# A recurrent mixer worked in two halves of four tiles inside one long fp32 transformer kernel

## The reference, cut to what matters

```python
def recurrent_mixer(h, w_in, conv_w, conv_b, w_a, b_a, w_x, b_x, lam, w_out):
    gate, xr = jnp.split(h @ w_in, 2, axis=-1)
    gate = jax.nn.gelu(gate, approximate=True)
    xr = causal_conv(xr, conv_w, conv_b)              # 4 taps along the tokens
    return (rg_lru(xr, w_a, b_a, w_x, b_x, lam) * gate) @ w_out

def rg_lru(x, w_a, b_a, w_x, b_x, lam):               # w_a, w_x: 8 blocks of 128 x 128
    r = sigmoid(blockwise(x, w_a) + b_a)
    i = sigmoid(blockwise(x, w_x) + b_x)
    log_a = 8.0 * r * log_sigmoid(lam)
    a = exp(log_a)
    u = sqrt(-expm1(2.0 * log_a)) * (i * x)
    # scan along the tokens: h_t = a_t * h_(t-1) + u_t
```

## Time and profile before

| what | value |
|---|---|
| median of the three runs | 2420.32 us (2416.55 to 2423.21) |
| the profiled execution's own time | 2414.51 us |
| its span, first to last instruction | 2413.1 us |
| TensorE busy | 2189.7 us, 91% of the span |
| VectorE busy | 1417.7 us, 59% |
| ScalarE busy | 1118.3 us, 46% |
| chain of waits that ended last | TensorE 78%, VectorE 14%, ScalarE 4% |
| mean granted TensorE clock | 0.957 of 2.4 GHz |
| the mixer, from its first transpose to its last matmul | about 2094.7 to 2207.8 us of the span |

### The profile page before, as it was taken

How to read it: one execution, slowest core, us unless ns; L and a number is a source line. 1 busy time by engine, 2 the same in 40 slices (tenths; PEclk the granted TensorE clock), 3 DMA queues, 4 the chain that set the end, 5 groups by cost and what they waited for, 6 DMA issues and landing times.

```text
span 2413.1 us, 25425 instructions
## 1 busy us (share of the span) xinstructions
PE 2189.7 (91%) x10080; PEld 1790.5 (74%) x10080; DVE 1417.7 (59%) x1934; ACT 1118.3 (46%) x1711; POOL 31.9 (1%) x40
## 2 busy tenths in 40 slices
PE   4998879999999878999989999988999999977998
PEld 3785667788778567778878878757788788755886
DVE  2795665555479565555545545765555555546553
ACT  2434435544444443544444445634544444464442
POOL 0000000000000000000000000100000000000000
PEclk8998899999999889999999999999999999998999
DMA  6553124455455312445545554322455455432553
GB/s 199 185 192 122 37 97 147 148 189 189 162 188 193 105 52 90 148 148 189 183 161 191 180 178 175 143 84 86 168 187 182 178 179 190 167 138 109 180 191 122
DMA packets 53277, 371.10 MB, mean 154 GB/s; under 512 B 6439, under 2 KB 6583, under 8 KB 9512
## 3 DMA queue, kind: packets, MB, share of 16 engines
q1 hardware_dynamic: 49248, 358.19, 41.3%
q0 software_dynamic: 1552, 4.20, 0.9%
q10 hardware_dynamic: 2360, 7.09, 0.8%
HBM read 366.31 MB, written 3.15 MB: 153 GB/s over the span
## 4 chain that ended last, share of the span: by engine, by line
PE 78%; DVE 14%; ACT 4%; DMA 2%; issue 1%; POOL 0%; ACTq 0%; DVEq 0%; POOLq 0%
PE ps L434 22%; PE ps L436 22%; PE ps L435 22%; DVE ring_lo L957 4%; DVE acc L1160 3%; PE ps L479 3%; PE ps L528 2%; DMA skew<-acc 2%; PE ps L625 1%; PE ps L684 1%; PE ps L463 1%; PE ps L513 1%; ACT upper_w L1582 1%; ACT z L1638 1%; DVE xn L1092 1%
## 5 line engine op out<-in xcount | busy, mean ns | idle before, releaser
L957 DVE TENSOR_TENSOR ring_lo<-ring,upper_w 128x1024 fp32r<-128x1024 f32 x659 | 804.4, 1229 | 537.7 <-ACT upper_w L1582 533.2
L1582 ACT CAST upper_w<-ring 128x1024 fp32r<-128x1024 f32 x659 | 689.8, 1055 | 582.9 <-PE ps L436 579.3
L434 PE MATMUL ps<-upper_w,nT_hi 128*128 128x512 f32 x1992 | 791.6, 397 | 70.1 <-DVE nT_lo L1540 24.9
L435 PE MATMUL ps<-ring_lo,nT_hi 128*128 128x512 f32 x1992 | 779.5, 391 | 0.0
L436 PE MATMUL ps<-upper_w,nT_lo 128*128 128x512 f32 x1824 | 713.1, 391 | 0.0
L434 PEld LDWEIGHTS ps<-upper_w,nT_hi 128*128 128x128 f32 x1992 | 379.9, 191 | 151.0 <-DVE ring_lo L957 29.9
L435 PEld LDWEIGHTS ps<-ring_lo,nT_hi 128*128 128x128 f32 x1992 | 379.5, 191 | 76.4 <-issue 1.0
L436 PEld LDWEIGHTS ps<-upper_w,nT_lo 128*128 128x128 f32 x1824 | 345.5, 189 | 73.1
L436 PE MATMUL ps<-upper_w,tT_lo 128*128 128x512 f32 (+1 forms) x792 | 309.5, 391 | 0.0
L434 PE MATMUL ps<-upper_w,z_hi 128*128 128x512 f32 x624 | 244.3, 391 | 2.7 <-DVE x L1015 2.7
L435 PE MATMUL ps<-ring_lo,z_hi 128*128 128x512 f32 x624 | 242.8, 389 | 0.0
(11 more groups left out here) (288 smaller groups left out, 1423.6 us busy)
## 6 DMA issues: line engine op xcount, KB each, us to landing
ring<-in_w SPq DMA_DIRECT2D x340, 1024.0 KB, 4.8
big<-in_gains ACTq DMA_DIRECT2D x6, 512.0 KB, 3.7
skew<-acc POOLq DMA_DIRECT2D x1, 2048.0 KB, 46.5
z<-in_mem ACTq DMA_DIRECT2D x2, 1024.0 KB, 6.5
big<-skew POOLq DMA_DIRECT2D x1, 1536.0 KB, 7.8
x<-in_x SPq DMA_DIRECT2D x1, 1024.0 KB, 4.9
out<-x ACTq DMA_DIRECT2D x2, 512.0 KB, 3.1
const<-in_const SPq DMA_DIRECT2D x1, 593.0 KB, 6.3
```

What stands on the lines that cost most here:

```text
L434: PE.matmul(out, hi, w_hi, start=start, stop=False)
L435: PE.matmul(out, hi, w_lo, start=False, stop=False)
L957: V.tensor_tensor(ring_lo[:, q % RING, cols], ring[:, q % RING, cols], upper_w[:, n % AHEAD, :].bitcast(F32), ALU.subtract).then_inc(*lo_c ...
L1582: A.copy(upper_w[:, n % AHEAD, :], ring[:, q % RING, part * HALF:(part + 1) * HALF]).then_inc(*hi_cut.up(h))
```

## The change

The reference and the layout of the inputs stay. What changes lies in the three engines' `recurrent` functions and in the list of the ring's chunks:

- The weights of the sigmoids leave the ring. ScalarE's queue loads them, 1 MB, into `xn`, which is free there, as `gate_w`. The ring has 339 chunks where it had 340.
- Convolution, sigmoids, decay, square root, scan and gelu are done for tiles 0 to 3 (index 0) and tiles 4 to 7 (index 1). Their steps stand as `beside` work between the cuts of `rec.in1`, `rec.in2`, `rec.in3` and the output product. TensorE turns tiles 0 to 3 of the x part behind the first half of `rec.in1`, tiles 4 to 7 behind the first half of `rec.in2`; the eight block matmuls of index 0 stand behind the second half of `rec.in2`, those of index 1 and the first gelu turn behind the first half of `rec.in3`, and the second gelu turn behind the second half of the output product.
- All four taps of the convolution are VectorE's. Exp and tanh take the decay factor as their scale, tile by tile, in place of VectorE's product (L1522).
- The output product has its chunks in another order: input tiles 0 to 3 for columns 0 to 511 (`rec.out0a`) and 512 to 1023 (`rec.out1a`), then tiles 4 to 7 for both (`rec.out0b`, `rec.out1b`).
- The cut-ahead goes on from `rec.in3` into the output product.

The diff, cut to its core (first the chunks, then TensorE, VectorE, ScalarE):

```diff
         w.add(f"rec.in{b}", [at + 2 * b, at + 2 * b + 1])
-    w.end_run("ffn_a.up0", "rec.in3")
-    w.add("rec.gates", [at + 8], split=False)
-    for b in range(2):
-        w.add(f"rec.out{b}", [at + 9 + 2 * b, at + 10 + 2 * b])
+    w.gates = at + 8
+    for part in range(2):
+        for b in range(2):
+            w.add(f"rec.out{b}{'ab'[part]}", [at + 9 + 2 * b + part])
     ffn_stream(w, "ffn_d", at + 13)
-    w.end_run("rec.out0", "ffn_d.down")
+    w.end_run("ffn_a.up0", "ffn_d.down")
...
+    gate_w = xn[:, :, :].rearrange("p t n -> p (t n)")
...
+        def gemm(seg, lhs, banks, ready=(), beside=None, first=0, kts=None):
+
+            if first == 0:
+                free(*banks)
+            kts = kts or 2 * len(W.span[seg])
             for c, h in enumerate(W.span[seg]):
                 w_hi, w_lo = weights(h)
                 for k in range(2):
-                    f, cols = 2 * c + k, slice(k * BLK, (k + 1) * BLK)
+                    f, cols = first + 2 * c + k, slice(k * BLK, (k + 1) * BLK)
...
+            def inputs(i):
+                turn(f"rec.cin{i}", cols_of(z, D + 512 * i), 4, [act_out.at(f"rec.in{i}")], lambda c: act_out.at(f"rec.cin{i}.{c}"))
+
+            def gates(i):
+
+                PE.wait_ge(*gates_loaded.at("gates"))
+                PE.wait_ge(*dve_out.at(f"rec.conv{4 * i + 3}"))
+                free(4, 5, 6, 7)
+                for kind in range(2):
+                    for j in range(4):
+                        c = 4 * i + j
+                        m = PE.matmul(ps[:, 4 + 2 * kind + j // 2, j % 2 * T:(j % 2 + 1) * T], gate_w[:, (8 * kind + c) * P:(8 * kind + c + 1) * P], xT[:, c, :], start=True, stop=True)
+                m.then_inc(*psum_full.up(f"rec.gates{i}"))
+                for j in range(4):
+                    held(act_out.at(f"rec.s{i}.{2 * j + 1}"), 4 + j)
+
+            def gelus(i, banks):
+                turn(f"rec.g{i}", cols_of(z, 512 * i), 4, [act_out.at(f"rec.in{2 + i}")], lambda c: act_out.at(f"rec.g{i}.{c}"), banks=banks)
+            gemm("rec.in0", lhs, (0, 1), n)
+            held(act_out.at("rec.in0"), 0, 1)
+            gemm("rec.in1", lhs, (2, 3), beside=lambda c: inputs(0) if c == 0 else None)
+            held(act_out.at("rec.in1"), 2, 3)
+            work = {0: lambda: inputs(1), 1: lambda: gates(0)}
+            gemm("rec.in2", lhs, (0, 1), beside=lambda c: work.get(c, lambda: None)())
+            held(act_out.at("rec.in2"), 0, 1)
+            gemm("rec.in3", lhs, (2, 3), beside=lambda c: (gates(1), gelus(0, (0, 1))) if c == 0 else None)
+            held(act_out.at("rec.in3"), 2, 3)
             ready = [dve_out.at(f"rec.lo{c // 4}") for c in range(8)]
-            gemm("rec.out0", lhs, (0, 2), ready)
-            gemm("rec.out1", lhs, (1, 3))
+            for part in range(2):
+                for b in range(2):
+                    if b and not part:
+                        gelus(1, (6, 7))
+                    gemm(f"rec.out{b}{'ab'[part]}", lhs, (b, b + 2), ready, first=4 * part, kts=KT)
...
-            if h + AHEAD - 1 <= W.run_end[h]:
-                cut(h + AHEAD - 1)
+            n = W.halves[h][2] + AHEAD - 1
+            if n < len(W.split) and W.split[n] <= W.run_end[h]:
+                cut(W.split[n])
...
+            def conv(c):
+                if c % 4 == 0:
+                    V.wait_ge(*act_out.at(f"rec.cin{c // 4}.2"))
+                if c == 0:
+                    V.wait_ge(*pool_out.at("rec.left"))
+                w = s2("rw")
+                V.tensor_scalar(xT[:, c, :], cin8[:, c, 0:T], w[:, 4 * c:4 * c + 1], s2("rb")[:, c:c + 1], ALU.mult, ALU.add).then_inc(*dve_out.up())
+                for k in range(1, 4):
+                    own()
+                    V.scalar_tensor_tensor(xT[:, c, :], cin8[:, c, k:k + T], w[:, 4 * c + k:4 * c + k + 1], xT[:, c, :], ALU.mult, ALU.add).then_inc(*dve_out.up(f"rec.conv{c}" if k == 3 else None))
+
+            def squared(i):
+                part = parts8[i]
+                V.wait_ge(*act_out.at(f"rec.s{i}.7"))
+                own()
+                V.tensor_tensor(iT[:, part, :], iT[:, part, :], xT[:, part, :], ALU.mult).then_inc(*dve_out.up())
+                V.wait_ge(*act_out.at(f"rec.th{i}"))
                 V.tensor_tensor(rT[:, part, :], aT[:, part, :], aT[:, part, :], ALU.mult).then_inc(*dve_out.up())
                 own()
+                V.scalar_tensor_tensor(th[:, part, :], rT[:, part, :], 1.0, th[:, part, :], ALU.add, ALU.mult).then_inc(*dve_out.up(f"rec.sq{i}"))
+
+            def scanned(i):
+                part = parts8[i]
+                V.wait_ge(*act_out.at(f"rec.root{i}"))
                 V.tensor_tensor(iT[:, part, :], iT[:, part, :], th[:, part, :], ALU.mult).then_inc(*dve_out.up())
                 own()
                 for c in range(part.start, part.stop):
                     V.tensor_tensor_scan(rT[:, c, :], aT[:, c, :], iT[:, c, :], 0.0, ALU.mult, ALU.add).then_inc(*dve_out.up())
                 own()
+                V.wait_ge(*act_out.at(f"rec.g{i}.2"))
+                V.tensor_tensor(nT[:, part, :], rT[:, part, :], gT[:, part, :], ALU.mult).then_inc(*dve_out.up(f"rec.h{i}"))
+
+            def rest(i):
+                part = parts8[i]
+                V.wait_ge(*act_out.at(f"rec.hi{i}"))
+                V.tensor_tensor(nT_lo[:, part, :], nT[:, part, :], nT_hi[:, part, :].bitcast(F32), ALU.subtract).then_inc(*dve_out.up(f"rec.lo{i}"))
+
+            def last_conv():
+                conv(6)
+                conv(7)
+            cuts("rec.in0")
+            work = {1: lambda: conv(0), 2: lambda: conv(1), 3: lambda: conv(2)}
+            cuts("rec.in1", lambda n: work.get(n, lambda: None)())
+            work = {0: lambda: conv(3), 1: lambda: conv(4), 2: lambda: conv(5), 3: last_conv}
+            cuts("rec.in2", lambda n: work[n]())
+            work = {1: lambda: squared(0), 3: lambda: scanned(0)}
+            cuts("rec.in3", lambda n: work.get(n, lambda: None)())
+            rest(0)
+            squared(1)
+            work = {2: lambda: scanned(1), 3: lambda: rest(1)}
+            for n, h in enumerate(h for part in "ab" for b in range(2) for h in W.span[f"rec.out{b}{part}"]):
+                cut_ahead(h)
+                work.get(n, lambda: None)()
...
+            def rows_of(seg, b, bank):
+                A.wait_ge(*product(seg))
+                scaled(f"rec.in{b}", block_of(z, (2, 3, 0, 1)[b]), ps[:, bank:bank + 2, :])
+
+            def inputs(i):
+                for c in (0, 2):
+                    pair_to(f"rec.cin{i}", c, cin8[:, 4 * i + c:4 * i + c + 2, 3:3 + T], 6 + c // 2)
+
+            def gates(i):
+                A.wait_ge(*psum_full.at(f"rec.gates{i}"))
+                for kind in range(2):
+                    for j in range(4):
+                        c = 4 * i + j
+                        dst, bias = (rT, s2("ba", c, c + 1)) if kind == 0 else (iT, s2("bx", c, c + 1))
+                        A.activation(dst[:, c, :], ps[:, 4 + 2 * kind + j // 2, j % 2 * T:(j % 2 + 1) * T], ACT.Sigmoid, bias=bias).then_inc(*act_out.up(f"rec.s{i}.{4 * kind + j}"))
+
+            def decays(i):
+                own()
+                for c in range(4 * i, 4 * i + 4):
+                    A.activation(aT[:, c, :], rT[:, c, :], ACT.Exp, scale=lam[:, c:c + 1]).then_inc(*act_out.up())
+                for c in range(4 * i, 4 * i + 4):
+                    A.activation(th[:, c, :], rT[:, c, :], ACT.Tanh, scale=lam[:, c:c + 1]).then_inc(*act_out.up(f"rec.th{i}" if c % 4 == 3 else None))
+
+            def gelus(i, bank):
+                for c in (0, 2):
+                    A.wait_ge(*psum_full.at(f"rec.g{i}.{c}"))
+                    A.activation(gT[:, 4 * i + c:4 * i + c + 2, :], ps[:, bank + c // 2, :].rearrange("p (c n) -> p c n", c=2), ACT.Gelu_apprx_tanh).then_inc(*act_out.up(f"rec.g{i}.{c}"))
+
+            def root(i):
+                part = parts8[i]
+                A.wait_ge(*dve_out.at(f"rec.sq{i}"))
+                A.activation(th[:, part, :], th[:, part, :], ACT.Sqrt, scale=-1.0).then_inc(*act_out.up(f"rec.root{i}"))
+
+            def upper(i):
+                part = parts8[i]
+                A.wait_ge(*dve_out.at(f"rec.h{i}"))
+                A.copy(nT_hi[:, part, :], nT[:, part, :]).then_inc(*act_out.up(f"rec.hi{i}"))
+
+            def first_root():
+                root(0)
+                gates(1)
+            A.dma_start(gate_w, io["w"][W.gates]).then_inc(*gates_loaded.up("gates", 16))
+            cuts("rec.in0")
+            A.wait_ge(*pool_out.at("rec.n.rstd"))
+            rows_of("rec.in0", 0, 0)
+            cuts("rec.in1", lambda n: inputs(0) if n == 0 else None)
+            rows_of("rec.in1", 1, 2)
+            work = {0: lambda: inputs(1), 2: lambda: gates(0)}
+            cuts("rec.in2", lambda n: work.get(n, lambda: None)())
+            rows_of("rec.in2", 2, 0)
+            work = {0: lambda: decays(0), 1: lambda: gelus(0, 0), 2: first_root}
```

(9 more changed lines are left out.)

86 lines of the change are left out of this document (5 added, 81 removed).

## The result

| | before | after |
|---|---|---|
| median | 2420.05 us (2416.55 to 2423.21, 4 runs) | 2406.49 us (2403.95 to 2408.61, 4 runs) |
| the profiled execution's own time | 2414.51 us | 2404.92 us |
| its span, first to last instruction | 2413.1 us | 2403.5 us |
| the mixer, first transpose to the first ACTIVATE of `post_norm` | 113.0 us | 101.8 us |

The ratio is 0.9944, with a 95% interval of 0.9926 to 0.9962: 13.6 us faster, where 11.6 were forecast. (A fourth run of the kernel before moved its median from 2420.32 to 2420.05 us.) The mixer is measured from 2094.74 to 2207.76 before and from 2097.56 to 2199.32 after; it gives 11.3 us.

What follows compares the result with a forecast made beforehand. TensorE bounds the kernel, busy 91% of the span, so only its standstills or half-clock stretches pay; 17.9 us earlier start less 3.6, 1.7 and 1.1 gives 11.6 us: 2402.9 profiled, 5.8 more for the median, 2408.7 us, range 2401 to 2417.

Steps and rivals of the forecast that it cites:

- The gap and what fills it: Between `rec.in3` and output product, 37.2 us before; turns and block matmuls move beside products, `rec.in3` ends 7.5 us later.
- The walk: Step-by-step timing of the changed mixer on the old profile's clock; ends at 2196.2 against 2207.76, 11.6 us less.
- The first rest: VectorE's `nT_lo` of tiles 0 to 3, ready at 2165.7; TensorE's wait of 24.9 us becomes 11.8.
- ScalarE decides: Before the output product, ScalarE's list runs from 2138.8 to 2157.2 and VectorE's scan stands behind its last cut.
- The output product: Last mixer product: slow first half 4.95 us, fourth half ends 2180.0, second wait 3.6 us, then 1.7 us of clock.
- The unknown price: Exp or tanh of 128x256 with per-channel scale on ScalarE: 0.40 us each, 3.3 us for eight, 4.1 by the dearer row.
- The sum: Mixer: 17.9 us from the earlier start, less 3.6 (second wait), 1.7 (its clock) and 1.1 (turn): 11.6 us less.
- A drain at each switch of table: Rival on ScalarE: 1.3 us idle around each table switch takes 7.1 of 11.6 us; 2416 us, shared chance 0.17.
- Half speed throughout: Rival on TensorE: waits leave the clock at 0.50 in `rec.in2`, `rec.in3` and output product; 2434 us, chance 0.07.
- Nearly all hidden: Rival: both rests come before TensorE asks, so 32 us go; 2389 us, chance 0.05.
- The order does not do what it says: Rival: VectorE or ScalarE holds the first rest until the second's work is done; 2416 us, within a shared chance 0.17.
- The gate weights and a ring chunk collide: Loading 1 MB on ScalarE's queue may delay a ring chunk some 5 us; 0 to 5 us, once, if uncovered.

Runs made afterwards that it cites:

- Experiment 2: Changed kernel with scan, upper part and rest of tiles 0 to 3 ahead of the cut for the output product's third half; mixer 96.0 us against 101.8.
- Experiment 3: Changed kernel with the output product in its old order, all input tiles for columns 0 to 511, then 512 to 1023; mixer 105.0 us against 101.8.
- Experiment 4: Changed kernel with useless fp32 matmuls in TensorE's two waits, 12 before the output product and 3 before its second half; mixer 98.8 us against 101.8.
- 5: Changed kernel with the chain of tiles 0 to 3 pulled forward and their output in `xn`; median 2392.60 us, ratio 0.9889 to the kernel before, mixer 89.3 us.
- 7: Changed kernel with tanh replacing the mixer's sigmoids, gelu and square root, leaving one table load of eight; mixer 98.7 us against 101.8.
- 9: Kernel of 5 with ScalarE's scaling of `rec.in3` ahead of two cuts, exp and tanh ahead of two more; median 2390.52 us, ratio 0.9873, mixer 88.5 us.
- experiment 8: Changed kernel with the convolution's first tap back on ScalarE, tile by tile; mixer 101.4 us against 101.8.
- Experiment 1: Kernel before with only gate weights on ScalarE's queue and cutting ahead continued from `rec.in3` into the output product; mixer 109.1 us, 3.9 less than before.

## Why the prediction was right

**The gap and what fills it.** The walk put the end of `rec.in3` 7.5 us later than before, at 2153.9. It ended at 2156.2, which is 2153.3 with the 2.8 us taken off, 7.0 us later than before. TensorE waited 0.96 us for tile 7, against 0.7. (The prediction's "9.5 us of turns and block matmuls" leaves out one turn: by its own prices three turns and 16 block matmuls are 10.6 us, and those are what the walk adds up.)

**The first rest.** The step "ScalarE decides" is what the traces show: one gap of 0.86 us on ScalarE (the sign to look for said none, the walk had 0.7), 6.07 us of idle on VectorE behind a cut, a wait of 11.9 us where the walk had 11.8. The rest was done at 2165.1 on the clock of before, where the walk had 2165.7; the wait agrees to 0.1 us because both of its ends came 0.5 to 0.6 us sooner. Experiment 2 shows that the order, not the length of the chain, makes half of it.

**The output product.** The second wait was 3.67 us (walk: 3.6), the fifth half slow by one stretch at half clock (1.7 us forecast; 4.70 us at a mean of 0.64 lose 1.7). Experiment 3 shows why the wait is not twice as long. Experiment 4 measured both restarts at 3.0 us; the prediction had 1.7 for the second, and left the first as it was before. There it was off: the clock was low for 5.9 us and not 4.5, which costs 0.7 us more. The product had started 0.5 us sooner than in the walk, so the fourth half still ended at 2180.0, as forecast. That is two misses that cancel.

**What decides the end.** The traces of experiments 2, 4, 5, 7 and 9 show what the walk holds but does not say: the mixer ends a fixed time after the second rest, for either state of the clock in the fifth half. From the first transpose, the second rest is done after 88.8 us in the changed kernel, 83.1 in experiment 2 and 85.7 in 7, and the mixer takes 12.9 to 13.0 us more (101.8, 96.0, 98.7), with a slow stretch in the fifth half. In experiments 4, 5 and 9 it is done after 87.4, 77.9 and 77.1 us, and the mixer takes 11.3 us more (98.8, 89.3, 88.5), at the full clock. (In experiment 8, with 6.1 us at the low clock, it was 14.2.) So in these kernels a shorter first wait helps only as far as it brings the second rest forward.

**The unknown price.** Four exp and four tanh took 2143.26 to 2146.56, 3.3 us, the value taken.

**The sum.** 11.6 forecast, 11.3 in the mixer's trace. After the mixer the profiled execution was 1.2 us shorter (204.2 against 205.3 us), but this stretch took 203.9 to 205.3 us in the eleven profiled executions, so that is scatter. The rest of the 13.6 us between medians lies within the interval. That the median came within 2.2 us of 2408.7 is partly luck. The forecast set the median 5.8 us above the profiled execution, as it was before; after, it lies 1.6 us above it (2404.92 us against 2406.49). The prediction had 2402.9 for the profiled one, which was 2.8 us late at the mixer.

**What the prediction didn't tell.** It counted the halves' early start as one term. Experiment 1 splits it: the uninterrupted run of cuts alone, with the gate weights out of the ring, gives the kernel before 3.9 us. Of the other 7.4 us, no run separates the halves of channels from the place of turns and block matmuls beside the products; that is argued from the walk and the trace. And the prediction held VectorE's lost decay products and added taps to be about even; experiment 8 bears it out for the tap to half a microsecond, and the decay product was not tried.

**The rivals.** *A drain at each switch of table*: no gap of that kind stands around the loads in the list above. The root ends at 2154.18, the load starts at 2154.20 and the first sigmoid at 2155.50, so a switch took 1.3 us. The rule of the Trainium skill ("ScalarE: Activation LUTs", "What ACT_TABLE_LOAD costs") adds about 1380 ns of drain to each load of 1283 ns. By these rows it does not hold here. *Half speed throughout*: in the mixer's products the clock was low in two stretches only, the two restarts. *Nearly all hidden*: false, though experiments 5 and 9 came to 2392.6 and 2390.5, near its 2389. (Its 32 us hold 4 us of clock, where the prediction itself had read a loss of 2.3.) *The order does not do what it says*: the first rest was done 18.5 us ahead of the second, so the second one's work did not hold it. *The gate weights and a ring chunk collide*: the load landed within 4.9 us, long before its use.

```profile
xn<-in_w ACTq DMA_DIRECT2D x1, 1024.0 KB, 4.9
```
